# Eight high products, then eight low ones, in every half of the joint weight stages

## The reference

```python
proj = n @ w_in
h = x + jnp.concatenate([gla_out, nsa_out], axis=-1) @ w_out
return h + (jax.nn.silu(m @ w_gate) * (m @ w_up)) @ w_down
...
x = x + gate * _rmsnorm(y @ w_out, post_g)
...
y = _multiscale_pool(proj[..., :POOL_WIDTH], pool_w, pool_scale) * jax.nn.silu(proj[..., POOL_WIDTH:])
```

## Time and profile before

| | |
|---|---|
| median of 3 runs | 1977.56 us (1975.25 to 1978.0) |
| the profiled execution's own time | 1974.55 us |
| its span, first to last instruction | 1972.9 us |
| mean granted TensorE clock | 0.994 |
| PE busy | 1936.8 us (98%) |
| DVE busy | 1591.0 us (81%) |
| ACT busy | 966.0 us (49%) |
| 16 DMA engines | 434.64 MB, mean 220 GB/s |

### The profile page before, as it was taken

The page is one execution under the profiler, slowest core; times in us unless marked ns, Lnnn a source line. Parts: engine busy times, 40 slices in busy tenths (PEclk is TensorE's granted clock), DMA queues, the critical chain, the costliest instruction groups (busy, mean ns, idle before and its releaser), DMA issues.

```text
span 1972.9 us, 38262 instructions
## 1 busy us (share of the span) xinstructions
PE 1936.8 (98%) x14274; PEld 1731.3 (88%) x14274; DVE 1591.0 (81%) x2186; ACT 966.0 (49%) x1458; POOL 214.5 (11%) x299
## 2 busy tenths in 40 slices
PE   7999999999999999999999999999999998999997
PEld 7998888998888888888888899887888887999986
DVE  6986777668888988889989878789988877678754
ACT  6553456555444444444444455246564455544453
POOL 1000000020000220002311111111100130000011
PEclk9999999999999999999999999999999999999999
DMA  7554653356777887777888875677657884568553
GB/s 243 171 172 140 207 189 113 124 171 220 234 236 243 274 306 235 236 236 252 287 288 309 303 250 173 204 243 239 202 179 242 271 284 155 180 204 288 190 191 129
DMA packets 121161, 434.64 MB, mean 220 GB/s; under 512 B 13248, under 2 KB 15680, under 8 KB 120784
## 3 DMA queue, kind: packets, MB, share of 16 engines
q1 hardware_dynamic: 92240, 328.11, 50.6%
q0 software_dynamic: 28800, 104.87, 15.9%
HBM read 430.83 MB, written 2.10 MB: 219 GB/s over the span
## 4 chain that ended last, share of the span: by engine, by line
PE 87%; DVE 7%; DMA 2%; issue 2%; ACT 1%; DVEq 0%; POOL 0%; POOLq 0%; SPq 0%; ACTq 0%
PE ps L677 17%; PE ps L680 17%; PE ps L678 17%; PE ps L663 8%; PE ps L664 8%; PE ps L665 8%; DVE w_lo L1751 3%; PE ps L814 2%; DMA side<-w_side 2%; PE ps L1153 1%; PE ps L1163 1%; PE ps L747 1%; PE ps L749 1%; PE ps L748 1%; DVE mod_odd L1768 1%
## 5 line engine op out<-in xcount | busy, mean ns | idle before, releaser
L1751 DVE TENSOR_TENSOR w_lo<-raw,w_hi 128x1024 fp32r<-128x1024 f32 x610 | 728.4, 1235 | 40.8 <-ACT w_hi L1307 40.2
L678 PEld LDWEIGHTS ps<-ba_act,w_lo 128*128 128x128 f32 x3264 | 613.3, 188 | 143.2 <-issue 1.2
L1307 ACT ACTIVATE w_hi<-raw 128x1024 fp32r<-128x1024 f32 x610 | 612.1, 1042 | 218.4 <-PE ps L665 156.1
L677 PE MATMUL ps<-ba_act,w_hi 128*128 128x512 f32 x1632 | 652.8, 400 | 1.6 <-DVE w_lo L1751 1.3
L680 PE MATMUL ps<-ba_act,w_hi 128*128 128x512 f32 x1632 | 645.6, 396 | 0.0
L678 PE MATMUL ps<-ba_act,w_lo 128*128 128x256 f32 x3264 | 641.8, 278 | 0.0
L677 PEld LDWEIGHTS ps<-ba_act,w_hi 128*128 128x128 f32 x1632 | 309.7, 190 | 6.6 <-issue 5.0
L680 PEld LDWEIGHTS ps<-ba_act,w_hi 128*128 128x128 f32 x1632 | 305.9, 187 | 0.0
L663 PE MATMUL ps<-ba_act,w_hi 128*128 128x256 f32 x912 | 262.0, 287 | 5.6 <-DVE w_lo L1751 5.1
L664 PE MATMUL ps<-ba_act,w_hi 128*128 128x256 f32 x912 | 258.9, 284 | 0.0
L665 PE MATMUL ps<-ba_act,w_lo 128*128 128x256 f32 x912 | 258.8, 284 | 0.0
(11 more groups left out here) (376 smaller groups left out, 1932.6 us busy)
## 6 DMA issues: line engine op xcount, KB each, us to landing
raw<-w_main SPq DMA_DIRECT2D x610, 512.0 KB, 4.4
side<-w_side POOLq DMA_DIRECT2D x200, 512.0 KB, 4.6
x_tok<-x_in SPq DMA_DIRECT2D x4, 512.0 KB, 6.2
ctx_tok<-ctx_tok SPq DMA_DIRECT2D x1, 2048.0 KB, 10.4
y_out<-res SPq DMA_DIRECT2D x4, 384.0 KB, 3.1
table<-counts_tab SPq DMA_DIRECT2D x1, 512.0 KB, 13.0
y_out<-res SPq DMA_DIRECT2D x2, 256.0 KB, 3.0
cons<-cons_in SPq DMA_DIRECT2D x1, 478.0 KB, 11.0
```

Of the source, the lines that this page charges most:

```text
L677: pe.matmul(ps[:, bank, :], wh, act[:, kt, :, :], start=first and b == 0, stop=False)
L678: mm = pe.matmul(ps[:, bank, 0:T], wl, act[:, kt, 0, :], start=False, stop=False)
L1307: act.activation(w_hi[:, slot, 0:n], raw[:, slot, 0:n], ACT.Copy).then_inc(hi_ready, 1)
L1751: dve.tensor_tensor(w_lo[:, slot, 0:n], raw[:, slot, 0:n], w_hi[:, slot, 0:n].bitcast(F32), ALU.subtract)\
```

## The change

In `joint_products` the two kinds of product are no longer interleaved: all eight H of a half come first, then all eight L. Ahead of the first L TensorE waits for `lo_ready`. Ahead of the first H it waits for `hi_ready` instead of `lo_ready`, except in the first two written-out steps of a stage (k < 2), where the wait for `lo_ready` ahead of the half stays.

```diff
-            def joint_products(bank, c, par, act, first, last, split=None):
+            def joint_products(bank, c, par, act, first, last, low, split=None):
 
                 slot = 2 * par + c
                 for b in range(8):
-                    wh, wl = w_hi[:, slot, b * P:(b + 1) * P], w_lo[:, slot, b * P:(b + 1) * P]
+                    wh = w_hi[:, slot, b * P:(b + 1) * P]
                     kt = 8 * c + b
                     if split is not None:
                         pe.wait_ge(S(split[0]), split[1] + kt + 1)
-                    if b % 2 == 0:
-                        pe.matmul(ps[:, bank, :], wh, act[:, kt, :, :], start=first and b == 0, stop=False)
-                    mm = pe.matmul(ps[:, bank, 0:T], wl, act[:, kt, 0, :], start=False, stop=False)
-                    if b % 2:
-                        mm = pe.matmul(ps[:, bank, :], wh, act[:, kt, :, :], start=False, stop=last and b == 7)
+                    pe.matmul(ps[:, bank, :], wh, act[:, kt, :, :], start=first and b == 0, stop=False)
+                pe.wait_ge(lo_ready, low)
+                for b in range(8):
+                    wl = w_lo[:, slot, b * P:(b + 1) * P]
+                    mm = pe.matmul(ps[:, bank, 0:T], wl, act[:, 8 * c + b, 0, :], start=False, stop=last and b == 7)
                 return mm
...
-                    pe.wait_ge(lo_ready, i * 4 + (2 * s + c + 1))
+                    ready = i * 4 + (2 * s + c + 1)
                     nb = min(8, kt - 8 * c)
                     waits = split[0] if split else None
                     if stage in JOINT:
-                        mm = joint_products(par, c, par, act, c == 0, c == 1, waits)
+                        pe.wait_ge(lo_ready if isinstance(i, int) and k < 2 else hi_ready, ready)
+                        mm = joint_products(par, c, par, act, c == 0, c == 1, ready, waits)
                     else:
+                        pe.wait_ge(lo_ready, ready)
                         mm = half_products(ps[:, par, 0:width], c, par, range(nb), *act, 8 * c, c == 0, c == 1, waits)
```

## The result

| | before | after |
|---|---|---|
| median of 13 runs | 1978.0 us | 1980.14 us |
| lowest to highest | 1975.25 to 1979.39 | 1977.75 to 1984.67 |
| profiled execution, time (span) | 1974.55 (1972.9) | 1978.91 (1977.2) |

The ratio of after to before is 1.0016, with a 95% interval of 1.0009 to 1.0023: the changed kernel is slower by 0.16%, some 3 us (the medians are 2.1 us apart). I had forecast 4 us less.

The account below looks back on a forecast made before the run. TensorE was taken as the bound nearly everywhere. The order's 4.1 us less 0.1 given back made 4.0 us off: 1970.6 for the profiled execution, 1973.6 us against the median; own range 1971 to 1976, wide range 1964 to 1984.

Parts of the forecast that it names:

- What bounds the kernel: Whole kernel: TensorE busy 1936.8 of 1972.9 us; joint stages' waits for low weights only 1.3 us together.
- The order: Joint products: runs of eight H and eight L shorten each half by 0.010 us, 4.1 us over 408 halves.
- runs of L pay, runs of H don't gain: Rival, joint products: H stays 0.2333 us, L takes 0.120; 16.3 us slower, 1993.9 us; chance 10%.
- The rival from the issue gap: Rival, joint products: order is indifferent, as the skill page's columns-plus-constant rule gives; 1977.6 us; chance 14%.
- The weight loads: Runs of eight L: each load hides behind only an L, costing 5 ns per L, already in the 0.120 us.
- The added wait: Ahead of each half's first L, 408 times: lo_ready has come, so 0; upper bound 33 us.
- The wait ahead of the first H: On hi_ready from a stage's third step: could win 1.3 us at most; taken as 0, other end 0.5 us.
- The tiles of the activations: First steps of five joint stages: H ask for tiles earlier, up to 4.8 us if late; taken as 0.
- What is given back: down0, down1 and attention stages: gain partly lost to DVE and ACT; 0.1 us, other end 1.3.

Follow-up runs that it names:

- runs_of_16: Kernel before, reordered: a step's first half eight H then eight L, its second eight L then eight H; waits as before; ratio 0.9996.
- alternate: Kernel before with H and L strictly in turn, sixteen changes of width in a half, waits as before; ratio 1.0048.
- runs of 4: Kernel before with four H, four L, four H, four L in a half, waits as before; ratio 1.0036.
- wait alone: Kernel before, old order H L L H, with the change's relaxed wait and lo_ready ahead of the first L; 1977.63 us, ratio 1.0005.
- order alone: Changed kernel (eight H, then eight L) with the earlier wait for lo_ready ahead of every half; 1978.14 us against 1976.77, ratio 1.0007.
- moved_before: Kernel before with the last two side products of up2b moved into down2's first two steps; 1975.64 us, ratio 0.9991.
- small_side_after: Changed kernel with up2b's side weights loaded only in their first 64 of 1024 columns; 1976.08 us, ratio 0.9995 to the kernel before.

## Why the prediction was wrong

The time, 1980.14 us, fell into the wide range (1964 to 1984) and outside the case's own (1971 to 1976), on the wrong side of no change: +0.16% where I said -0.2%. That the wide range held it is no merit of the mechanism, which had the wrong sign. Step by step:

- *What bounds the kernel* held: TensorE, and the wait for the low weights is too small to matter.
- *The order* is the step that failed, in its term "I put 0.0017 on a change of width". The two paces of a run were right: 16 H and 16 L in runs_of_16 take 5.57 us, of which 16 x 0.3467 are 5.547. The price of a change was taken from the mix, less, and moved to long runs. There it is (2.793 - 2.7733) / 2 = 0.010 us, six times as much: in `down0` the first five H of a run take 0.228 to 0.236 us, only the last three the 0.227. By the sum over all joint products the term became +1.9 us instead of -4.1. The step behind it failed too, to give a change of width a price at all: in alternate the same sixteen changes cost 0.05 us a half in `down0` and nothing in `up1`. The rival "runs of L pay, runs of H don't gain" named the right sign and the point from which it decides, an H above 0.2279 us; it is 0.2300 on average, but by a slow start of each run and not by every H, so its 16.3 us were far too much.
- *The rival from the issue gap*: runs of 4 and alternate are 0.36% and 0.48% slower with the same columns, so the order is not indifferent. The rule of the Trainium skill ("TensorE: Matmul & The Clock Gate", Back-to-back issue gap) gives a warm product its columns plus a small constant and has no term for its neighbours. The trace does not agree: the same H takes from 0.227 to 0.236 us within one run of eight.
- *The weight loads*: eight L in a run took 0.95 us, 0.119 each, as the earlier trace rows said. Right.
- *The added wait* at 0: right, by the order and the wait alone.
- *The wait ahead of the first H* at 0, with 0.5 as the other end: the 0.5 us in `up2b` are gone in the profile, but order alone, without the relaxed wait, has only 0.24 left there, and moved_before has 1.2. A value between 0 and 1 us was right; the profiles don't say which.
- *The tiles of the activations* in the joint stages: no idle time there, right. But the one tile that was late belongs to `down2`, which is no joint stage and which I didn't look at. Its 0.52 us of waiting, behind a VectorE that waits for side loads, was in the trace of before. In the seven profiled kernels with these loads and products unmoved the wait is between 0.5 and 2.5 us, a wider span than the change moves; order alone (1.54 us) and the wait alone (1.65 us) each show it too. Whether it is what makes the runs of before spread over 4 us is not shown, since small_side_after and moved_before spread over 5.3 us without it.
- *What is given back*: 0.1 us was too little in the one profile (more was waited in `down2` than had gone in `up2b`); for the medians it can't be told from the swings.

Of the 3 us of the ratio, some 2 us are shown as the pace: 1.5 to 2.1 us in four pairs of traces that have the same difference of order. Whether the rest is a greater share of executions with the late tile and the low clock, or chance, stays open.

## What to carry to other kernels

When the bound is an engine that never idles, its pace per product is the first thing to measure, and a pace found at one pattern of neighbours is not a price list for another: by the same sum a change of width cost six times as much behind runs of eight as in groups of two, and in alternation it cost nothing in one stage and most in the next. A pace read in one stage is no price for all stages either: sum the whole trace. Try the orders on the chip before grouping for a wait that nobody waits for. And look for the engine that is nearly late: a stall of 0.5 us in the trace of before was up to 2.5 us in other kernels, and moving two instructions off that path took it away; the median fell by 1.3 us, with an interval that just reaches no change.

## What the runs showed of the hardware that I had not expected

- The same products with the same columns differ by up to 2% with their order: in `down0` 2.785 us a half in runs of 16, 2.793 in runs of 8, 2.81 in runs of 4, 2.787 in runs of 2, 2.83 in alternation.
- The same order, H and L in turn, has two paces in one execution: 2.83 us a half in `down0`, 2.775 in `up1`.
- The low clock does not follow the length of the idle time by itself: 1.54 us of waiting had 3.4 us at 0.50 behind it, and so had 1.03 us (runs_of_16); 1.65 us in another kernel had none. By the starts, such a stretch costs about 1.5 us in the changed kernel.
- A wait for a semaphore that has come costs TensorE nothing that shows, 408 times over: all joint products take 1148.5 us with it (wait alone) and 1148.6 without.
